# Attention steps of ScalarE and VectorE placed ahead of the take's evacuation

## The reference, cut to what matters

```python
s = jnp.where(mask[None, :, None, None, :, :], s, NEG_INF_2)
p = jax.nn.softmax(jnp.concatenate([s, sink], axis=-1), axis=-1)[..., :-1]
o = jnp.einsum('bnkgqs,bnskd->bnqkgd', p.astype(v.dtype), vw)
```

## Time and profile before

| | us |
|---|---|
| median of 3 runs | 1220.14 (1219.16 to 1221.27) |
| profiled execution, its own time | 1216.97 |
| its span, first to last instruction | 1214.8 |
| busy PE, DVE, ACT | 1079.9, 838.6, 671.2 |
| mean granted clock of PE | 0.942 |

### The profile page before, as it was taken

The page is one execution under the profiler, slowest core; times in us unless marked ns, Lnnn a source line. Parts: engine busy times, 40 slices in busy tenths (PEclk is TensorE's granted clock), DMA queues, the critical chain, the costliest instruction groups (busy, mean ns, idle before and its releaser), DMA issues.

```text
span 1214.8 us, 16346 instructions
## 1 busy us (share of the span) xinstructions
PE 1079.9 (89%) x6089; PEld 930.8 (77%) x6089; DVE 838.6 (69%) x1516; ACT 671.2 (55%) x1324; POOL 71.1 (6%) x46
## 2 busy tenths in 40 slices
PE   5789798769599999999988899999887889999887
PEld 4668686668588887787877888888766888888766
DVE  5566553456559999999975866686567766587654
ACT  5345374524378988788854487523335378633233
POOL 0100200000010101003000000100101000010100
PEclk9989798879689999999999999999898999999889
DMA  8522124304149999999964322332243322332220
GB/s 333 173 104 105 57 83 162 115 36 174 36 162 398 348 379 365 351 381 369 388 233 161 134 105 104 139 139 105 88 156 130 144 108 105 143 135 105 88 86 35
DMA packets 30034, 211.44 MB, mean 174 GB/s; under 512 B 3328, under 2 KB 3712, under 8 KB 4992
## 3 DMA queue, kind: packets, MB, share of 16 engines
q1 hardware_dynamic: 28368, 205.01, 45.1%
q10 hardware_dynamic: 1584, 5.34, 1.2%
HBM read 209.28 MB, written 1.05 MB: 173 GB/s over the span
## 4 chain that ended last, share of the span: by engine, by line
PE 59%; DVE 21%; ACT 9%; DMA 5%; issue 4%; POOL 2%; SPq 0%; DVEq 0%; POOLq 0%
PE ps L484 15%; PE ps L486 14%; PE ps L485 14%; DVE w_lo L383 9%; DMA ring<-in_panels 5%; PE ps L489 4%; PE ps L925 3%; ACT s_buf L1737 3%; PE ps L633 2%; ACT L1737 2%; POOL stat L395 2%; DVE gates L383 1%; PE ps L691 1%; DVE scr L383 1%; DVE op_lo L383 1%
## 5 line engine op out<-in xcount | busy, mean ns | idle before, releaser
L383 DVE TENSOR_TENSOR w_lo<-ring,w_hi 128x512 fp32r<-128x512 f32 x760 | 488.4, 700 | 201.0 <-ACT w_hi L1690 200.2
L1690 ACT ACTIVATE w_hi<-ring 128x512 fp32r<-128x512 f32 x760 | 424.8, 620 | 249.5 <-PE ps L486 216.2
L484 PE MATMUL ps<-w_hi,op_hi 128*128 128x512 f32 (+2 forms) x928 | 370.5, 399 | 21.6 <-DVE w_lo L383 13.4
L485 PE MATMUL ps<-w_lo,op_hi 128*128 128x512 f32 (+2 forms) x928 | 361.5, 390 | 0.0
L486 PE MATMUL ps<-w_hi,op_lo 128*128 128x512 f32 (+2 forms) x928 | 361.5, 390 | 0.0
L484 PEld LDWEIGHTS ps<-w_hi,op_hi 128*128 128x128 f32 x928 | 177.9, 192 | 63.3 <-DVE w_lo L383 22.2
L486 PEld LDWEIGHTS ps<-w_hi,op_lo 128*128 128x128 f32 x928 | 177.3, 191 | 36.4
L485 PEld LDWEIGHTS ps<-w_lo,op_hi 128*128 128x128 f32 x928 | 177.9, 192 | 32.0
L484 PE MATMUL ps<-op_hi,w_hi 128*128 128x256 f32 x448 | 134.5, 300 | 8.2 <-DVE op_lo L383 8.2
L485 PE MATMUL ps<-op_lo,w_hi 128*128 128x256 f32 x448 | 130.5, 291 | 0.0
L486 PE MATMUL ps<-op_hi,w_lo 128*128 128x256 f32 x448 | 130.2, 291 | 0.0
(11 more groups left out here) (226 smaller groups left out, 1059.1 us busy)
## 6 DMA issues: line engine op xcount, KB each, us to landing
ring<-in_panels SPq DMA_DIRECT2D x194, 1024.0 KB, 6.4
cst<-in_c ACTq DMA_DIRECT2D x1, 1219.0 KB, 5.3
buf_a<-in_pre ACTq DMA_DIRECT2D x2, 512.0 KB, 6.2
keys<-in_post ACTq DMA_DIRECT2D x2, 512.0 KB, 3.6
out<-x_tok SPq DMA_DIRECT2D x2, 512.0 KB, 2.6
cst<-in_c ACTq DMA_DIRECT2D x1, 960.0 KB, 7.0
x_tok<-in_x SPq DMA_DIRECT2D x1, 512.0 KB, 4.7
x_tok<-in_x ACTq DMA_DIRECT2D x1, 512.0 KB, 4.9
```

What stands on the lines that cost most here:

```text
L383: return V.tensor_tensor(o, a, b, op)
L484: T.matmul(o, l[0], r[0], start=start, stop=False)
L485: T.matmul(o, l[0], r[1], start=False, stop=False)
L1690: return A.activation(o, a, ACT.Copy, scale=scale)
```

## The change

`behind` is split in two. `ahead(t)` does `feed` and then those attention steps that are named; `behind(t)` does the others after the evacuation, as before. For ScalarE `turn_out` and `scores_out` go ahead, for VectorE `scores_out` alone. PE, POOL and SP keep their order.

```diff
@@ ScalarE (the same in VectorE's program, with ("scores_out",) for the names)
+            def ahead(t):
+                feed(2 * t + AHEAD)
+                for name, arg in beside.get(t, ()):
+                    if name in ("turn_out", "scores_out"):
+                        table[name](arg)
+
             def behind(t):
                 for name, arg in beside.get(t, ()):
-                    if name in table:
+                    if name in table and name not in ("turn_out", "scores_out"):
                         table[name](arg)
...
             for t in range(T_Z, T_GATE):
-                feed(2 * t + AHEAD)
+                ahead(t)
...
                 for t in range(t0, t0 + L2_TAKES - 3):
-                    feed(2 * t + AHEAD)
+                    ahead(t)
                     r = t - t0
```

More of the change, by code:

```diff
@@ L1580, in dve_program @@
                      "att_turn": lambda l: back_los(l, 0), "hg_turn": lambda l: back_los(l, 1)}
+            def ahead(t):
+                feed(2 * t + AHEAD)
+                for name, arg in beside.get(t, ()):
+                    if name in ("scores_out",):
+                        table[name](arg)
             def behind(t):
                 for name, arg in beside.get(t, ()):
-                    if name in table:
+                    if name in table and name not in ("scores_out",):
                         table[name](arg)
```

## The result

The changed kernel takes 1234.59 us (median of 4 runs, 1230.57 to 1235.43), the one before 1219.65 on the same chip (4 runs, 1217.41 to 1221.27): a ratio of 1.0115, 95% interval 1.0097 to 1.0134. It is slower, by 14.9 us between the medians, outside the range given.

A forecast was written before the change was run, and what follows sets the result against it. PE was taken as the bound, stopping before turns until the exponent ends, with rings setting the new rounds. First layer -3.0 and attention ends +2.2 gave -0.8 us: 1220.14 to 1219.3 us, range 1213 to 1224.

The forecast's parts named there:

- The end of the attention: Layers 2 and 3: the last turned job's copy delays take 29's evacuation, so take 30 starts 1.1 us late in each.
- the ring: Layers 2 and 3: exponent, table load, evacuation, `w_hi`, `w_lo`, mask, maxima, next exponent; sets rounds of 9.32 or 10.12 us.
- The term +2.2: End of attention in layers 2 and 3: take 30 late by 1.1 us in each, 2.2 us slower together.
- the first kind: Attention rounds with one evacuation (takes 13, 19, 21), forecast at 9.32 us each.
- The end at take 30: End of attention in layers 2 and 3: take 30 was to start 1.1 us late in each.
- The first layer: First layer: fewer PE stops, followed round by round, give a lead of 3.0 us at turn 11, kept afterwards.
- Table loads: ScalarE: six more loads of 1.3 us, 7.8 us in all, counted in rings or ahead of evacuations, otherwise falling into waits.
- The rival of a switch at twice that: ScalarE: a table switch after an exponent costs twice its row, each ring 1.3 us longer, 1237 us; chance 2%.
- The rival on the slower side: Rings longer than the rows say, through VectorE's queue; at 0.4 us more a ring, 1225 us; chance 18%.
- The clock rival: First layer, 187 to 200 and 245 to 259: one or both clock falls go away, 1213.2 to 1216.9 us; chance 25%.
- The rival that the rings do not bind: Layers 2 and 3: PE keeps its own round of 8.78 us, giving 1202.5 us; chance 4%.

The follow-up runs named there:

- e1: Changed kernel, but in take 25 of layers 2 and 3 ScalarE evacuates first again, as before the change: 1215.77 us, ratio 0.9972.
- e7: Changed kernel with ScalarE's take 25 of layers 2 and 3 back, and VectorE's scores ahead of `feed` in those layers: 1207.27 us, ratio 0.9894.
- e8: Changed kernel whole, take 25 included, with VectorE's scores ahead of `feed` in layers 2 and 3: 1214.16 us, ratio 0.9940.
- e4: Kernel before, with ScalarE's new order only in take 25 of layers 2 and 3: 1231.93 us, ratio 1.0095.
- e6: Kernel before, with ScalarE's new order everywhere except take 25 of layers 2 and 3, VectorE's order old: 1228.16 us, ratio 1.0065.
- e10: Changed kernel with ScalarE's take 25 of layers 2 and 3 back, and VectorE's scores ahead of `feed` everywhere: 1199.48 us, ratio 0.9822.
- e9: Kernel before, with VectorE's new order everywhere and its scores ahead of `feed` in layers 2 and 3, ScalarE's order old: 1219.88 us, ratio 0.9987.

## Why the prediction was wrong

**The step that failed** is the one headed *The end of the attention*, with the sentence before it, that the last turn starts where it did. In layers 2 and 3 I priced the evacuation only at take 29, the last, and in the rounds as a member of the ring. For the takes between I took it that PE never waits for a bank. I had not looked at when each bank is next filled. For take 25 the answer is: by the next take, in twelve matmuls, because the kind of the takes changes there. The term +2.2 for the two layers was in truth +14.9: from the matmul that stood at 684.02 to take 30 the lateness grows from 2.3 to 9.7 us, and in layer 3 from 10.2 to 17.7. The stop and what stands behind it make 9.6 and 9.5 of this, 6.3 of stop in each and the rest matmuls at half clock; the first turn and the rounds ahead give some 2 back in each, which I had at nothing. In the runs the one take is worth 18.8 us (changed kernel, 1234.59, less e1).

**The rings were right.** Predicted 9.32 and 10.12 us; the exponents of the changed kernel start at 739.77 and 749.88, 10.11 apart, and the turns of jobs 0 and 1 are 9.13 apart, of jobs 1 and 2 10.18, of jobs 3 to 5 9.33 and 9.34. Of the first kind one round was 0.19 under the sum and two were on it. What I had wrong is who stops: PE waited for the values (0.9 us, twice), not for the turn, because VectorE empties the bank of the values behind the maxima. With take 25 undone one round is no ring any more: in e1 the last two exponents start at 746.96 and 754.39, 7.43 apart, since no evacuation stands between them. There take 30 starts at 761.25, 2.5 us before its old time, of which 0.7 was there when the layer began: 1.8 us gained in a layer, where I had 1.1 lost.

**The end at take 30** was 0.16 us late, not 1.1.

**The first layer** had the right end, lead 2.95 at turn 11 against 3.0 forecast, and 3.53 against 3.6 at the transfer. In between the agreement is in part luck: the lead was 3.1 at turn 9 (forecast 2.3), 2.0 at the up projection (1.45) and 1.0 at the values, where the start at 245.8 had it at -0.2; the turn then started 2.6 us behind the values and not 1.35, in matmuls at half clock. "Which the rest of the layer keeps" was right in the main (3.2 at the matmul that stood at 275), but the kernel does not: 1.6 us of it are in the time.

**Table loads** were seen as 1.28 us with the next instruction 0.01 to 0.02 us behind (751.86, 753.15), also behind an exponent. The rival of a switch at twice that is out. The Trainium skill, ScalarE: Activation LUTs, section What ACT_TABLE_LOAD costs, has a drain of 1380 ns on top; no row here shows one, and the turns 10.18 us apart leave it no room.

**The rival on the slower side** had the right sign and another place: VectorE's queue was named, ScalarE's in one take decided. The clock rival came true for one of its two places, 0.89 for 0.76 behind the panel, and not for the other (0.62 for 0.63 in 245 to 259); what decided was the clock behind a stop that the change makes. In its price for the second place the idle time is 4.0 by the earlier trace rows (14.00 less 10.04) and not 3.0, which makes it 3.2 us for 3.7. The rival that the rings do not bind was refuted for this change, and e7 makes it true by moving `w_lo` out of the ring.

Open: why the half clock in the router lies as it does, and how much of a first-layer lead survives it in general.

## What to carry to other kernels

When an evacuation is moved behind something slow, ask of every bank separately who fills it next and how soon, and look hardest at the seam where one kind of loop follows another: there the slack of the regular rounds is not to be had. A ring through two engines' queues could be summed from rows here to 0.1 us in most rounds, and the same sum showed a member that could be moved out of it. Take the one bad instance of a reorder back and keep the others; here that turned 1.2% slower into 0.3% faster, moving `w_lo` out of the ring in layers 2 and 3 made it 1.1%, and in the first layer too 1.8%.

## What was not expected of the hardware

A stop of PE can cost more than its length, through the clock behind it. Stops of 1.0 us left the granted clock at 1.00. Behind 2.69 us (e8) it was 0.57 over the next 4 us and soon back. Behind 4.25 and 6.32 us (e4 and the changed kernel) it was 0.50 for at least 9 us, in both alike. From the matmul ahead of the 6.32 us stop to take 30 the price was 9.6 us.

Length alone does not decide it. In e6 half clock stands behind the stop of 1.83 us shown above and behind those of 1.81 (762.19) and 1.76 us (1026.44), while behind those of 1.77 us at 1015.72 and 1.81 us at 1057.06 the granted clock is 1.00 for the next 8 us.

In the first layer less stop went with more clock: in e10, without the stop of 3.05 us ahead of it, the clock in 245 to 259 was 0.88 instead of 0.63. But it is not that stop alone. e9 has it (3.06 us, ahead of the values at 244.53), and its row for the same stretch is:

```profile
245.00:259.00 14.00, 12.53 (x79) 11.80 (x79) 5.46 (x11) 3.15 (x7) 0.00 (x0) 0.76 0.20 77
```
